# Eight-output units in an f32r-split encoder step: one eviction moved, two outputs in other banks, three sums in two passes

## What is computed

```
n  = RMSNorm(h);  z = n @ w_in -> q | k | v | u | g_a | g_b
A  = windowed attention with sinks (q, k, v)
B  = multi-scale causal pooling of u, minus u; one linear map per channel group; a scale
h += (sigmoid(g_a) * (A @ w_branch_a) + sigmoid(g_b) * (B @ w_branch_b)) @ w_out
h += relu(RMSNorm(h) @ w_up)^2 @ w_down                      (hidden width 8192)
h += sigmoid(RMSNorm(h) @ w_ple_gate) * RMSNorm(p @ w_ple_proj)
y  = RMSNorm(h)
```

## Time and profile before

| | |
|---|---|
| device time, median of 3 runs | 1683.36 us (1682.65 to 1683.42) |
| the profiled execution's own time | 1683.38 us |
| its span, first to last instruction | 1681.6 us |
| mean granted TensorE clock | 0.996 |
| PE busy | 1659.2 us (99% of the span) |
| DVE, ACT, POOL busy | 853.3, 669.9 and 83.8 us (51%, 40%, 5%) |
| the chain that ended last | PE 97%, DVE 2% |

### The profile page before, as it was taken

The page is one execution under the profiler, slowest core; times in us unless marked ns, Lnnn a source line. Parts: engine busy times, 40 slices in busy tenths (PEclk is TensorE's granted clock), DMA queues, the critical chain, the costliest instruction groups (busy, mean ns, idle before and its releaser), DMA issues.

```text
span 1681.6 us, 29214 instructions
## 1 busy us (share of the span) xinstructions
PE 1659.2 (99%) x11298; PEld 1650.8 (98%) x11298; DVE 853.3 (51%) x1179; ACT 669.9 (40%) x972; POOL 83.8 (5%) x76
## 2 busy tenths in 40 slices
PE   7999999999999999999999999999999999999997
PEld 7999999999999999999999999999999999999997
DVE  7577544444445556443344443344433544565765
ACT  6355534333333444443234433334333344444442
POOL 3034000000000003000000000000000300000000
PEclk9999999999999999999999999999999999999998
DMA  7533544444444444444444444444444444444431
GB/s 283 171 118 126 196 149 150 148 149 150 149 150 158 150 150 151 150 150 150 150 150 150 149 147 148 147 151 147 147 148 147 149 148 150 148 149 150 151 125 62
DMA packets 37961, 252.48 MB, mean 150 GB/s; under 512 B 5281, under 2 KB 6689, under 8 KB 8481
## 3 DMA queue, kind: packets, MB, share of 16 engines
q1 hardware_dynamic: 35136, 245.59, 41.1%
q10 hardware_dynamic: 2784, 6.35, 1.0%
HBM read 248.65 MB, written 3.27 MB: 150 GB/s over the span
## 4 chain that ended last, share of the span: by engine, by line
PE 97%; DVE 2%; ACT 0%; DMA 0%; issue 0%; POOL 0%; DVEq 0%; SPq 0%; POOLq 0%; ACTq 0%
PE acc L404 32%; PE acc L405 32%; PE acc L406 32%; PE s_ps L456 1%; DVE w_lo L811 0%; DMA h<-in_x 0%; PE o_ps L434 0%; PE t_ps L443 0%; DVE h L1162 0%; DVE sumsq L876 0%; ACT xa_hi L602 0%; DVE xa_lo L867 0%; ACT w_hi L581 0%; POOL prob_t L343 0%; PE m_ps L418 0%
## 5 line engine op out<-in xcount | busy, mean ns | idle before, releaser
L581 ACT ACTIVATE w_hi<-raw 128x1024 fp32r<-128x1024 f32 x462 | 487.4, 1059 | 882.5 <-PE acc L406 878.9
L404 PE MATMUL acc<-xa_hi,w_hi 128*128 128x320 f32 x2112 | 655.6, 310 | 9.1 <-DVE xa_lo L867 9.1
L405 PE MATMUL acc<-xa_lo,w_hi 128*128 128x320 f32 x2112 | 653.6, 309 | 0.0
L406 PE MATMUL acc<-xa_hi,w_lo 128*128 128x320 f32 x2112 | 653.6, 309 | 0.0
L811 DVE TENSOR_TENSOR w_lo<-raw,w_hi 128x1024 fp32r<-128x1024 f32 x462 | 550.5, 1232 | 19.3 <-ACT w_hi L581 19.0
L404 PEld LDWEIGHTS acc<-xa_hi,w_hi 128*128 128x128 f32 x2112 | 397.5, 188 | 9.9 <-DVE w_lo L811 9.3
L405 PEld LDWEIGHTS acc<-xa_lo,w_hi 128*128 128x128 f32 x2112 | 397.5, 188 | 0.2
L406 PEld LDWEIGHTS acc<-xa_hi,w_lo 128*128 128x128 f32 x2112 | 397.4, 188 | 0.0
L404 PE MATMUL acc<-xb_hi,w_hi 128*128 128x320 f32 x1280 | 395.8, 309 | 0.0
L405 PE MATMUL acc<-xb_lo,w_hi 128*128 128x320 f32 x1280 | 395.5, 309 | 0.0
L406 PE MATMUL acc<-xb_hi,w_lo 128*128 128x320 f32 x1280 | 395.5, 309 | 0.0
(11 more groups left out here) (161 smaller groups left out, 943.6 us busy)
## 6 DMA issues: line engine op xcount, KB each, us to landing
raw<-in_weights SPq DMA_DIRECT2D x229, 1024.0 KB, 4.8
h<-in_x SPq DMA_DIRECT2D x4, 640.0 KB, 8.0
h<-in_x ACTq DMA_DIRECT2D x1, 2560.0 KB, 12.8
raw<-in_weights SPq DMA_DIRECT2D x4, 512.0 KB, 9.2
out_y<-h ACTq DMA_DIRECT2D x2, 800.0 KB, 3.5
bias<-in_alibi SPq DMA_DIRECT2D x1, 512.0 KB, 11.3
out_y<-h ACTq DMA_DIRECT2D x1, 480.0 KB, 2.6
p_raw<-in_p_in ACTq DMA_DIRECT2D x1, 320.0 KB, 2.8
```

What stands on the lines that cost most here:

```text
L404: nc.tensor.matmul(out, w_hi[:, at:at + P], x_hi[:, m * T:(m + 1) * T], start=k == 0, stop=False)
L405: nc.tensor.matmul(out, w_hi[:, at:at + P], x_lo[:, m * T:(m + 1) * T], start=False, stop=False)
L406: mm = nc.tensor.matmul(out, w_lo[:, at:at + P], x_hi[:, m * T:(m + 1) * T], start=False, stop=k == depth - 1)
L581: nc.scalar.activation(w_hi[:, dst:dst + HALF], raw[:, src:src + HALF], ACT.Copy).then_inc(hi_done, 1)
```

## The change

Three edits, independent of each other:

- In `U_POOL`, DVE evicts output 1 before `pool_mean(7)` and `pool_low(7)`; these now stand ahead of output 2 (`c == 2`). ACT's order stays: `d_hi` of chunk 7 was already ahead of its `b_hi` of output 2.
- In `U_P0` and `U_P1`, outputs 4 and 5 go to `t_ps` and `o_ps` without a wait on `taken`. Outputs 6 and 7 stay in `acc[2]` and `acc[3]` and wait as before.
- Sums 1, 2 and 3 are made from an f32r pair: ACT copies the tile to `part_hi` (f32r), DVE subtracts to get `part_lo`, and PE multiplies a matrix of ones in f32r by both. DVE fills that matrix `ones_r` once, ahead of the out projection. For sum 1 `part_high` is on ACT after its last output chunk and `part_low` on DVE between the copies of outputs 1 and 2 of `U_P0`. For sum 2 both stand after the last up unit (on ACT behind the wait for all `xb_lo`). For sum 3 both stand after the last down unit, ahead of the next weight split. PE's sums stay where they are in its list.

```diff
--- before.py
+++ after.py
@@ -191,7 +191,8 @@
         p_hi, p_lo = sb("p_hi", KP * T, F32R), sb("p_lo", KP * T, F32R)
         e_sq = sb("e_sq", T)
         last_var, last_r = sb("last_var", NL), sb("last_r", NL)
-        sb("unused", 4 * KA * T - KD * T - 3 * KP * T - T - NL * 2)
+        part_hi, part_lo, ones_r = sb("part_hi", T, F32R), sb("part_lo", T, F32R), sb("ones_r", P, F32R)
+        sb("unused", 4 * KA * T - KD * T - 3 * KP * T - 3 * T - P - NL * 2)
         with ExitStack() as early:
             pline = sb("pline", 2 * PL, F32, early)
@@ -233,6 +234,7 @@
         acc = [psum(f"acc{i}") for i in range(BANKS)]
         s_ps, t_ps, o_ps, m_ps = psum("s_ps"), psum("t_ps"), psum("o_ps"), psum("m_ps")
         sums = (m_ps, s_ps)
+        embed_spare = {4: t_ps, 5: o_ps}
         raw_in = [sem(f"raw_in{i}") for i in range(RAW)]
@@ -256,6 +258,7 @@
         xadd, xodd = sem("xadd"), sem("xodd")
         n_mm = sem("n_mm")
         n_var = sem("n_var")
+        part_h, part_l = sem("part_h"), sem("part_l")
         n_first = sem("n_first")
         n_std = sem("n_std")
         n_r = sem("n_r")
@@ -384,7 +387,7 @@
         @block.tensor
         def _(pe):
-            def unit(u, parity, chunk, bank, depth, x_hi, x_lo, moving=None, ready=None, inner=False):
+            def unit(u, parity, chunk, bank, depth, x_hi, x_lo, moving=None, ready=None, inner=False, spare={}):
@@ -394,12 +397,12 @@
                     half = t // 8
                     if t % 8 == 0:
                         pe.wait_ge(lo_done, 2 * u + (half + 1))
-                    if k == 0 and not (isinstance(chunk, int) and chunk + o < BANKS):
+                    if k == 0 and o not in spare and not (isinstance(chunk, int) and chunk + o < BANKS):
                         pe.wait_ge(taken, chunk + (o - BANKS + 1))
                     if ready:
                         ready(o, k)
                     at = (2 * parity + half) * HALF + (t % 8) * P
-                    out = acc[(bank + o) % BANKS][:, 0:T]
+                    out = spare.get(o, acc[(bank + o) % BANKS])[:, 0:T]
                     m = moving(o, k) if moving else k
                     nc.tensor.matmul(out, w_hi[:, at:at + P], x_hi[:, m * T:(m + 1) * T], start=k == 0, stop=False)
                     nc.tensor.matmul(out, w_hi[:, at:at + P], x_lo[:, m * T:(m + 1) * T], start=False, stop=False)
@@ -417,6 +420,14 @@
                 for i, src in enumerate(sources):
                     mm = nc.tensor.matmul(sums[n % 2][:, 0:T], ones[:, :], src,
                                           start=i == 0, stop=i == len(sources) - 1)
+                mm.then_inc(n_mm, 1)
+
+            def split_sum(n):
+
+                pe.wait_ge(part_l, n)
+                pe.wait_ge(n_var, n - 1)
+                for i, part in enumerate((part_hi, part_lo)):
+                    mm = nc.tensor.matmul(sums[n % 2][:, 0:T], ones_r[:, :], part[:, :], start=i == 0, stop=i == 1)
                 mm.then_inc(n_mm, 1)
             def step(i):
@@ -501,11 +512,10 @@
             def embed(u, chunk):
                 unit(u, u % 2, chunk, 0, KP, p_hi, p_lo, moving=lambda o, k: k,
-                     ready=lambda o, k: pe.wait_ge(el, k + 1), inner=True)
+                     ready=lambda o, k: pe.wait_ge(el, k + 1), inner=True, spare=embed_spare)
             embed(U_P0, C_P0)
-            pe.wait_ge(fa, 2 + KD)
-            partition_sum(1, sumsq[:, :])
+            split_sum(1)
             def up_down(u0, c0, n, at, between=None):
@@ -526,8 +536,7 @@
             embed(U_P1, C_P1)
             def embedding_sum():
-                pe.wait_ge(e_add, KD)
-                partition_sum(2, esum[:, :])
+                split_sum(2)
             up_down(U_LAST, C_LAST, (FB - 1) * KF, U_LAST, embedding_sum)
@@ -537,8 +546,7 @@
             for s in range(4):
                 gate(U_GATE, s, (lambda o, k: pe.wait_ge(fl, KD + k + 1)) if s == 0 else None)
                 if s == 0:
-                    pe.wait_ge(fa, 2 + 2 * KD)
-                    partition_sum(3, sumsq[:, :])
+                    split_sum(3)
             with fours(pe, U_GATE + 4, UNITS) as u:
                 for s in range(4):
                     gate(u, s)
@@ -587,6 +595,12 @@
             def ahead(u, at, halves=range(2)):
                 split(u + AHEAD, at + AHEAD, halves)
+
+            def part_high(n, of, done, count):
+                act.wait_ge(done, count)
+                if n > 1:
+                    act.wait_ge(n_mm, n)
+                nc.scalar.activation(part_hi[:, :], of[:, :], ACT.Copy).then_inc(part_h, 1)
             def root(n, var, out, cols=T):
                 act.wait_ge(n_var, n + 1)
@@ -735,6 +749,7 @@
                 nc.scalar.activation(p_hi[:, tt(k)], p_raw[:, tt(k)], ACT.Copy).then_inc(eh, 1)
             out_chunks(KD - 4, KD)
+            part_high(1, sumsq, fa, 2 + KD)
             ahead(U_P0, U_P0)
             root(1, sumsq, r)
@@ -757,6 +772,7 @@
             ahead(U_P1, U_P1)
             up(U_LAST, C_LAST, (FB - 1) * KF, U_LAST)
             act.wait_ge(ul, 2 + FB * KF)
+            part_high(2, esum, e_add, KD)
             def last_down(first, end):
                 with fours(act, first, end) as i:
@@ -768,6 +784,7 @@
             last_down(0, 4)
             root(2, esum, re)
             last_down(4, KD)
+            part_high(3, sumsq, fa, 2 + 2 * KD)
             ahead(U_GATE, U_GATE)
             root(3, sumsq, r)
@@ -845,6 +862,10 @@
                 nc.vector.scalar_tensor_tensor(out=f, in0=v, scalar=1.5, in1=f,
                                                op0=ALU.add, op1=ALU.mult).then_inc(n_r, 1)
                 dve.wait_ge(n_r, 4 * n + 4)
+
+            def part_low(n, of):
+                dve.wait_ge(part_h, n)
+                nc.vector.tensor_tensor(part_lo[:, :], of[:, :], part_hi[:, :], ALU.subtract).then_inc(part_l, 1)
             def clear_sum(n):
@@ -1000,7 +1021,7 @@
                 if c < KA - 1:
                     step(u - U_STEP)
             for c in range(KA):
-                if c == 1:
+                if c == 2:
                     pool_mean(KA - 1)
                     pool_low(KA - 1)
                 if c == 4:
@@ -1057,6 +1078,7 @@
                 dve.wait_ge(fa, n + 2)
                 nc.vector.tensor_tensor(sumsq[:, :], sumsq[:, :], duo(sq, parity), ALU.add).then_inc(fa, 1)
+            nc.vector.memset(ones_r[:, :].bitcast(F32), 1.0)
             dve.wait_ge(h_in, 16)
             def out_chunks(first, end):
                 with fours(dve, first, end) as i:
@@ -1076,8 +1098,11 @@
             def embed(u, n):
                 for o in range(KD // 2):
+                    if n == 0 and o == 2:
+                        part_low(1, sumsq)
                     small_ready(dve, used, full, u, 1 + n, o)
-                    nc.vector.tensor_copy(e[:, tt(n * (KD // 2) + o)], acc[o % BANKS][:, 0:T]).then_inc(taken, 1)
+                    of = embed_spare.get(o, acc[o % BANKS])
+                    nc.vector.tensor_copy(e[:, tt(n * (KD // 2) + o)], of[:, 0:T]).then_inc(taken, 1)
                     if o % 4 == 3:
                         ahead(u, u, [o // 4])
@@ -1108,6 +1133,8 @@
             embed(U_P1, 1)
             up(U_LAST, C_LAST, (FB - 1) * KF, U_LAST)
+            part_low(2, esum)
+
             def last_down(first, end):
                 with fours(dve, first, end) as i:
                     for s in range(4):
@@ -1122,6 +1149,7 @@
             last_down(4, 8)
             newton(2, esum, re)
             last_down(8, KD)
+            part_low(3, sumsq)
             ahead(U_GATE, U_GATE)
             factor(3, sumsq, r)
             clear_sum(2)
```

## The result

The changed kernel takes 1688.2 us (median, 1688.0 to 1688.56), the kernel before beside it 1682.82 us: 1.0032 times as long, 95% interval 1.0023 to 1.0041. It is slower by 5.4 us. The profiled execution took 1688.02 us, 4.6 us more than the profiled one before.

A forecast was written before the change was run, and what follows sets the result against it. PE, busy 1659.2 of 1681.6 us, was taken to bound the kernel. Gains of 0.40, 0.35, 0.15, 0.25 and 0.25 against 4.60 gave +3.2; with 2.2 for the clock, 1683.38 became 1688.8 us, range 1686.0 to 1690.3.

The forecast's parts named there:

- U_POOL, -0.40: In U_POOL, PE's wait shrinks and moves from output 5 to output 6; output 7 starts at 181.83 instead of 182.22.
- U_P0 and sum 1, -0.35: Outputs 4 and 5 wait for nothing, sum 1 gets shorter; MLP starts at 642.53 instead of 642.88, ends 0 and -0.75.
- U_P1, -0.15: In U_P1, two matmuls that took 0.44 us take the 0.29 due, and DVE's copies keep their times.
- Sum 3, -0.25: After the last down unit, the pair is ready before PE asks; only the shorter sum counts, 0.54 to 0.29 us.
- Sum 2's wait, 4.5: Behind the last up unit PE waits for part_l from 1438.55 to 1443.04, 4.5 us, plus 0.1 restart.
- The rival in which its operands are in time: At sum 2 the pair is ready when PE asks; only gains of 1.4 us stay, 1682.0 us; chance 0.05.
- The clock, 2.2, with 0.1 for the restart: Sum 2's pause lowers PE's clock; recovery costs +2.2 us as at the kernel's start, ends 0 and 4.4; restart 0.1 separately.
- The rival that the clock holds: PE stalls at sum 2 but the clock does not fall: 1686.6 us, +0.19%; chance 0.25.
- The short sums do not get short: An f32r pass against ones takes 0.27, half a float32 sum: +0.5 on any case; a term, given no chance.

The follow-up runs named there:

- the unread matmuls: The changed kernel plus 28 PE matmuls of 320 columns, results never read, ahead of sum 2: 1685.98 us.
- that of 2.2 us: The changed kernel plus 14 PE matmuls with unread results ahead of sum 2: 1687.17 us; once more, one execution, 1686.39 us.
- those of 1.2 and 0.2 us: The changed kernel plus PE matmuls with unread results ahead of sum 2: 1685.85 us with 21 of them, 1685.98 us with 28.

## Why the prediction was right

It said 1688.8 us in a range of 1686.0 to 1690.3, slower; measured 1688.2. It said +5.4 us; the medians differ by 5.4, the two profiled executions by 4.6. That the medians meet the 5.4 is luck: the steps add up to 4.6, and the kernel before has a median of 1682.82 beside the result where the prediction had started from 1683.38. The mechanism, a wait at sum 2 and a lower clock behind it, was the one forecast. Step by step, in the profiled executions:

- **U_POOL, -0.40**: 182.95 to 182.57 with the unit's start 0.02 later, 0.40. The wait went to output 6 at 180.85, to the hundredth.
- **U_P0 and sum 1, -0.35**: the MLP's second matmul went from 643.03 to 642.19, 0.84 with `U_POOL`'s 0.38 in it, so -0.46. Two terms were off and nearly cancelled. `part_lo` was taken at 0.43, which no row gives (`d_lo` took 0.49), and took 0.83 beside POOL, so output 6 was freed later. The split was taken at its old 1.73, beside POOL's add, and took 1.21, because it now began at 640.14, just as that add ended, so the fifth copy freed the MLP in time.
- **U_P1, -0.15**: the first MLP matmul behind it went from 1325.90 to 1324.92; 0.98 less the 0.84 is 0.14.
- **Sum 3, -0.25**: 0.29 us for 0.54, and nothing waited for the pair.
- **Sum 2's wait, 4.5**: 4.44, made of the very steps named. The rival in which its operands are in time fell; moved midway (1681.22), they are.
- **The clock, 2.2, with 0.1 for the restart**: 1.68 in all, about 0.2 of it the restart and 1.5 the clock. This is the mis-sized term: the price was taken from the kernel's start, 4.94 us of slow matmuls, and here the clock was low for about 3.4. The start itself is no fixed price: in the kernel after, the matmuls there are 0.27 apart only until 11.91, not 14.04. Nor is the end, from which the fall was argued: it came 2.0 us after the last dense matmul before, and 2.1 to 5.1 us after it in the other eleven profiles, in some of them with the last six matmuls in between. The rival that the clock holds fell in all four profiles with the full pause, and the unread matmuls show that the pause is what lets it fall.
- **The short sums do not get short** fell: 0.29 at sums 1, 2 (midway) and 3.

Sum: -0.40 - 0.46 - 0.14 - 0.25 - 0.25 + 4.44 + 1.68 = +4.62, and the span grew by 4.6.

The Trainium skill's rule (TensorE: Matmul & The Clock Gate, "Terms") of half the throttled time gives an estimate of 1.7 us for the 3.4 us at the lower level; the rows give about 1.5 without the restart, so this case stays a little below the rule here as at the start (2.2 against 2.5).

## What to carry to other kernels

An operand that another engine makes is ready when that engine's list comes to the step, not when the step's inputs are there. Before a step is put behind a loop, look at which engine asks first: PE asks at its last up matmul, while DVE finishes that unit's work over 3 us later, a latency that had been free because nobody asked for it. In a kernel that is 99% PE, a pause of PE can be paid twice, once as time and once as clock: the pause of 4.3 us was in all four profiles, that of 2.2 us in one of two, and those of 1.2 and 0.2 us in neither of theirs. Against that, a sum in cheaper passes was worth 0.25 us. And a median can agree with a forecast whose terms do not: the check is the sum of the steps in the trace.

## What the runs showed that had not been expected

- A pause of 2.2 us brought the half rate in one execution and not in another of the same kernel, and the fall came over a microsecond after PE had begun to work again (1.2 by the granted clock, 1.3 by the spacing, 1441.85 to 1443.14). The times of that kernel spread over 2.0 us. Whether the full pause always brings it is open too: three executions without a trace, one with `U_POOL`'s mean later (1686.79 us) and two with `U_P0` reordered (1686.50 and 1686.65), have a mean granted clock of 0.997 where the others of these kernels have 0.995 or 0.996.
- DVE's subtraction of two SBUF tiles of 128x320 took 0.49 us alone, 0.83 us beside POOL's multiply and 0.99 us beside POOL's add. In both cases its end lies 0.34 to 0.35 us behind POOL's end (639.43 after 639.08, 640.47 after 640.13). The Trainium skill, SBUF — State Buffer, "Terms", says of the port pair shared by VectorE and GpSimd that the loser fully blocks until the other's instruction is done; these rows agree with that, and no run was made to test it.
- The last six matmuls of the kernel took 0.90, 1.15 or 1.56 us in different executions, and this is the clock too. In the kernel after and in the run with 28 unread matmuls (chain, then window):

```profile
1674.71 1.56 PE s_ps L569 x6
...
1674.00:1675.00 1.00, 0.29 (x1) 0.29 (x2) 0.56 (x4) 0.00 (x0) 0.00 (x0) 0.69 0.00 0
```

```profile
1672.97 0.90 PE s_ps L571 x6
...
1673.00:1674.00 1.00, 0.85 (x6) 0.71 (x6) 0.02 (x1) 0.00 (x0) 0.00 (x0) 0.95 0.00 0
```

By the means of 0.69 and 0.95 the level fell at about 1674.4, ahead of the six, and at 1673.9, behind them. In the kernel before it fell at 1669.6, ahead of its six at 1670.06, which took 1.56 us. With sum 2 in float32 it fell at 1669.2, among its six from 1668.74, which took 1.15. So the moment at which the clock falls moves single times of this kernel by up to 0.66 us without any edit; the two profiled executions that the account above compares both have 1.56.
